# Expert outputs weighted by slot and summed by accumulating stores, in a one-layer mixture-of-experts backbone kernel

## What is computed

```python
g_prob = softmax(t @ wg + bg)                 # 4 groups, the best one is taken
e_prob = softmax(e_logits of that group)      # 4 experts in it, the best two are taken
w = g_p * e_p / sum(e_p)                      # gate of each choice
hid = t @ w_exp_in[e]; a, up = split(hid)     # (1024 x 512) for each of 16 experts
y = (silu(a) * up * gate) @ w_exp_out[e]      # (256 x 1024)
x = layer_norm(ALPHA * x + gf * sum_of_two_y, ln2_g, ln2_b)
```

## Time and profile before

| | |
|---|---|
| runs | 552.16 us median of 3 (551.97 to 552.78) |
| profiled execution, first to last instruction | 550.5 us |
| what lies around the span, median minus span | 1.7 us |
| PE / DVE / ACT / POOL busy | 509.6 / 437.4 / 273.5 / 98.9 us |
| expert turns | about 356 to 509 us, some 9.35 us each |
| last normalisation | about 507 to 550 us |

### The profile page before, as it was taken

The page is one execution under the profiler, slowest core; times in us unless marked ns, Lnnn a source line. Parts: engine busy times, 40 slices in busy tenths (PEclk is TensorE's granted clock), DMA queues, the critical chain, the costliest instruction groups (busy, mean ns, idle before and its releaser), DMA issues.

```text
span 550.5 us, 8091 instructions
## 1 busy us (share of the span) xinstructions
PE 509.6 (93%) x3137; PEld 421.5 (77%) x3138; DVE 437.4 (79%) x703; ACT 273.5 (50%) x378; POOL 98.9 (18%) x114
## 2 busy tenths in 40 slices
PE   4999999999999997999999999999999999998670
PEld 1579999997799995777787788877888888886220
DVE  3217899989798803998559879989999999996984
ACT  2336412002031313997712224767888888884373
POOL 0005800003000001232000000212624242312201
PEclk9999999999999999999999999999999999999786
DMA  8997995729876551228188209989999999998667
GB/s 298 387 386 242 232 349 184 240 79 279 320 245 233 173 134 41 59 60 230 41 298 340 89 39 338 422 321 397 387 391 388 375 384 370 375 310 311 252 190 157
DMA packets 56831, 142.36 MB, mean 259 GB/s; under 512 B 8375, under 2 KB 17138, under 8 KB 50904
## 3 DMA queue, kind: packets, MB, share of 16 engines
q1 hardware_dynamic: 44792, 119.06, 60.3%
q0 software_dynamic: 9120, 20.80, 12.9%
q10 hardware_dynamic: 2880, 1.98, 1.2%
HBM read 129.71 MB, written 20.20 MB: 272 GB/s over the span
## 4 chain that ended last, share of the span: by engine, by line
PE 64%; DVE 18%; issue 7%; DMA 5%; ACT 3%; SPq 1%; DVEq 0%; POOL 0%; ACTq 0%; POOLq 0%
PE PS L1861 9%; PE PS L1863 9%; PE PS L1862 9%; PE PS L1959 8%; PE PS L1960 8%; PE PS L1964 8%; DVE PS L1391 2%; DMA uni<-in_w_ada 2%; PE PS L2266 2%; DMA g<-x_rows 2%; DVE w_lo L1525 2%; PE PS L2380 2%; DVE uni L1407 2%; ACT uni L948 1%; PE PS L2194 1%
## 5 line engine op out<-in xcount | busy, mean ns | idle before, releaser
L1861 PE MATMUL PS<-w_hi,act_hi 128*128 128x512 f32 x244 | 98.7, 405 | 0.9 <-DVE act_lo L1619 0.9
L1959 PE MATMUL PS<-act_hi,w_hi 128*128 128x320 f32 x320 | 97.6, 313 | 0.2 <-issue 0.2
L1960 PE MATMUL PS<-act_lo,w_hi 128*128 128x320 f32 x320 | 96.3, 309 | 0.0
L1863 PE MATMUL PS<-w_hi,act_lo 128*128 128x512 f32 x244 | 95.4, 391 | 0.0
L1862 PE MATMUL PS<-w_lo,act_hi 128*128 128x512 f32 x244 | 95.2, 390 | 0.0
L1281 DVE SCALAR_TENSOR_TENSOR uni<-raw,uni 128x512 f32<-128x512 f32 x112 | 75.1, 743 | 0.0
L1964 PE MATMUL PS<-act_hi,w_lo 128*128 128x320 f32 x320 | 72.9, 309 | 0.0
L1959 PEld LDWEIGHTS PS<-act_hi,w_hi 128*128 128x128 f32 x320 | 60.1, 188 | 4.2 <-issue 3.2
L1960 PEld LDWEIGHTS PS<-act_lo,w_hi 128*128 128x128 f32 x320 | 60.1, 188 | 0.0
L803 ACT ACTIVATE w_hi<-raw 128x2048 fp32r<-128x2048 f32 x14 | 26.4, 1915 | 58.5 <-PE PS L1964 48.3
L1861 PEld LDWEIGHTS PS<-w_hi,act_hi 128*128 128x128 f32 x244 | 45.9, 188 | 11.8 <-issue 1.9
(11 more groups left out here) (285 smaller groups left out, 934.2 us busy)
## 6 DMA issues: line engine op xcount, KB each, us to landing
raw<-in_w_ada SPq DMA_DIRECT2D x20, 1024.0 KB, 7.6
raw<-in_w_expert_in SPq DMA_DIRECT2D x16, 1024.0 KB, 11.8
uni<-in_w_expert_out SPq DMA_DIRECT2D x15, 1024.0 KB, 11.1
raw<-in_w_in SPq DMA_DIRECT2D x12, 1024.0 KB, 8.3
g<-in_w_expert_in SPq DMA_DIRECT2D x8, 1024.0 KB, 12.0
uni<-expert_rows SPq DMA_DIRECT2D x10, 512.0 KB, 7.2
uni<-in_w_ada SPq DMA_DIRECT2D x4, 1024.0 KB, 14.5
raw<-in_w_out SPq DMA_DIRECT2D x4, 1024.0 KB, 6.2
```

Of the source, the lines that this page charges most:

```text
L1861: T.matmul(out, lh, rh, start=first, stop=False)
L1863: return T.matmul(out, ll, rh, start=False, stop=last)
L1959: T.matmul(out, a, h_hi[:, k, sl], start=f, stop=False)
L1960: T.matmul(out, a, h_lo[:, k, sl], start=False, stop=False)
```

## The change

- The router's gates are computed earlier (`token_gates` in turn 0) and stored to a small DRAM array (`gate_dram`); for each expert POOL gathers the gates of its list entries into a column of `slot_gate` (`gather_gates`), and ACT's copy out of PSUM scales each row by it.
- `y_dram` becomes one array of 640 rows. SP zeroes it before attention. The expert stores add to it by token number.
- The expert in turn p is number (p % 4) * 4 + p // 4, so that the experts of a group are four turns apart, and the router's expert columns are permuted to match (also the bias, by one copy).
- Tokens are numbered with stride: token p of tile n is row 5p + n of `h2_dram` and `y_dram`.
- The end loads one row for each token (five loads), `weight_rows` and `add_rows` are gone, and the centring of a tile comes two tiles after its gating.

```diff
-    PAGE = 1024
+    PAGE = TOK
+        gate_dram = dram("choice_gates", (2 * PAGE, 1))
-        y_dram = dram("expert_rows", (2 * PAGE, D))
+        y_dram = dram("expert_rows", (TOK, D))
+        EXPERT = [(p % NG) * EG + p // NG for p in range(NE)]
+            sp.wait_ge(s_nb, 1)
+            for n in range(NT):
+                sp.dma_start(dap(y_dram, n * D, [[NT * D, P], [PAST, D // PAST], [1, PAST]]),
+                             no_bias.unsqueeze(1).to_broadcast([P, D // PAST, PAST])).then_inc(s_yz, 16)
             x1_away(1)
             expert_out(1)
+            sp.wait_ge(s_gt, 1)
+            sp.dma_start(dap(gate_dram, 0, [[NT, P], [PAGE, 2], [1, NT]]), gates[:, :, :]).then_inc(s_gd, 16)
             expert_in(5, 0)
-                for c in range(2):
-                    r0 = c * PAGE + t * P
-                    sp.dma_start(fin_y[:, n, c, :], y_dram[r0:r0 + P, :]).then_inc((s_fy, s_fy2)[c][n], 16)
+                sp.dma_start(fin_y[:, n, 0, :], dap(y_dram, n * D, [[NT * D, P], [1, D]])).then_inc(s_fy[n], 16)
+            def gather_gates(c):
+                if c == 0:
+                    pool.wait_ge(s_lc, 2)
+                    pool.wait_ge(s_gd, 16)
+                pool.indirect_dma_start(slot_gate[:, c:c + 1], None, gate_dram,
+                                        bass.IndirectOffsetOnAxis(ap=list_d[:, c:c + 1], axis=0),
+                                        bounds_check=2 * PAGE - 1, oob_is_err=False).then_inc(s_sg[c % 2], 16)
             def store_rows(c):
                 if c == 0:
-                    pool.wait_ge(s_lc, 2)
+                    pool.wait_ge(s_yz, 16 * NT)
                 pool.wait_ge(s_ya, c + 1)
-                pool.indirect_dma_start(y_dram, bass.IndirectOffsetOnAxis(ap=list_d[:, c:c + 1], axis=0), y_sb[:, c % 2, :], None,
-                                        bounds_check=2 * PAGE - 1, oob_is_err=False).then_inc(s_yst[c % 2], 16)
+                pool.indirect_dma_start(y_dram, bass.IndirectOffsetOnAxis(ap=list_s[:, c:c + 1], axis=0), y_sb[:, c % 2, :], None,
+                                        bounds_check=TOK - 1, oob_is_err=False, compute_op=ALU.add).then_inc(s_yst[c % 2], 16)
                 if 4 <= c < NE + 3:
                     store_rows(c - 4)
+                if 2 <= c < NE + 2:
+                    gather_gates(c - 2)
-                nc.scalar.activation(y_sb[:, b, :], PS[:, 6:8, :].rearrange("p a n -> p (a n)"), ACT.Copy).then_inc(s_ya, 1)
+                act.wait_ge(s_sg[b], 16 * (c // 2 + 1))
+                nc.scalar.activation(y_sb[:, b, :], PS[:, 6:8, :].rearrange("p a n -> p (a n)"), ACT.Copy,
+                                     scale=slot_gate[:, c:c + 1]).then_inc(s_ya, 1)
             expert_ohi(0)
             nc.scalar.activation(small[:, 100:101], eps, ACT.Tanh)
+            act.wait_ge(s_d12, 1)
+            nc.scalar.activation(uni[:, 9340:9340 + NG * NT], uni[:, 9340:9340 + NG * NT], ACT.Exp)
+            nc.scalar.activation(uni[:, 9360:9360 + NT], uni[:, 9360:9360 + NT], ACT.Exp).then_inc(s_d12, 1)
             half_tanh(0, 0)
             gathered_hi(1, 1)
             expert_whi(2, 0)
             act_hi_copy(0, 0)
-            act.wait_ge(s_d12, 1)
-            nc.scalar.activation(uni[:, 9340:9340 + NG * NT], uni[:, 9340:9340 + NG * NT], ACT.Exp)
-            nc.scalar.activation(uni[:, 9360:9360 + NT], uni[:, 9360:9360 + NT], ACT.Exp).then_inc(s_d12, 1)
...
-            act.wait_ge(s_slot, 1)
-            for n in range(3):
-                weight_rows(n)
             for n in range(NT):
-                if n == NT - 1:
-                    scaled_rows(n - 1)
                 squares(n)
                 deviation(n)
-                if n + 3 < NT:
-                    weight_rows(n + 3)
-                if 1 <= n < NT - 1:
-                    scaled_rows(n - 1)
+                if n >= 2:
+                    scaled_rows(n - 2)
+            scaled_rows(NT - 2)
...
+            V.memset(small[:, 8:25], 0.0)
             link(V.memset(uni[:, 5120:5200], 0.0))
+            dve.wait_ge(s_wrl, 64)
+            link(V.tensor_copy(rb[:, E_AT:NR].rearrange("p (j g) -> p g j", g=NG),
+                               logits[:, 0, 0:NE].rearrange("p (g j) -> p g j", g=NG)))
...
             silu_times_up(0, 0)
+            token_gates()
             gathered_lo(1, 1)
...
-            add_rows(0)
-            for n in range(NT + 1):
-                if n < NT:
-                    gate_rows(n)
-                    mean(n)
-                if n + 1 < NT:
-                    add_rows(n + 1)
-                if 1 <= n < NT:
-                    inverse(NT + n - 1)
-                    centred(n - 1)
+            for n in range(NT):
+                gate_rows(n)
+                mean(n)
+                if 2 <= n < NT - 1:
+                    final_inverse(n - 2)
+                    centred(n - 2)
+            last_residual()
+            for n in (NT - 3, NT - 2):
+                final_inverse(n)
+                centred(n)
             last_tile()
```

More of the change, by code:

```diff
@@ L1168, in _ @@
                     act.wait_ge(s_y, i + (NE + 1))
-                    nc.scalar.activation(y_sb[:, 1, :], PS[:, 6:8, :].rearrange("p a n -> p (a n)"), ACT.Copy).then_inc(s_ya, 1)
-            def weight_rows(n):
-                act.wait_ge(s_fy[n], 16)
-                y1 = fin_y[:, n, 0, :]
-                nc.scalar.activation(y1, y1, ACT.Copy, scale=gates[:, 0, n:n + 1]).then_inc(s_fg, 1)
+                    nc.scalar.activation(y_sb[:, 1, :], PS[:, 6:8, :].rearrange("p a n -> p (a n)"), ACT.Copy,
+                                         scale=over_gate).then_inc(s_ya, 1)
             def scaled_rows(n):
@@ L1656, in _, with token_gates @@
             for h in range(2):
-                V.tensor_scalar(list_last[:, h:h + 1], PS[:, 7, NE - 1:NE], 2.0, 2.0 * AWAY + h, ALU.mult, ALU.add)
+                link(V.tensor_scalar(list_t[:, NE + h:NE + h + 1], second[:, NE - 1:NE], 2.0, 2.0 * AWAY + h, ALU.mult, ALU.add))
+                V.scalar_tensor_tensor(out=list_last[:, h:h + 1], in0=PS[:, 7, NE - 1:NE], scalar=2.0,
+                                       in1=list_t[:, NE + h:NE + h + 1], op0=ALU.mult, op1=ALU.add)
             V.tensor_scalar(list_d[:, 0:NE], PS[:, 7, 0:NE], AWAY, None, ALU.add).then_inc(s_lc, 1)
+            def token_gates():
+                dve.wait_ge(s_d12, 2)
+                gw = rs[:, 170:170 + 3 * NT].rearrange("p (a t) -> p a t", a=3)
+                link(V.tensor_reduce(gw[:, 0, :], gexp, AX.X, ALU.add))
+                link(V.scalar_tensor_tensor(out=gw[:, 1, :], in0=d12, scalar=1.0, in1=gw[:, 0, :], op0=ALU.add, op1=ALU.mult))
+                link(V.reciprocal(gates[:, 0, :], gw[:, 1, :]))
+                V.tensor_tensor(gates[:, 1, :], gates[:, 0, :], d12, ALU.mult).then_inc(s_gt, 1)
             silu_times_up(0, 0)
+            token_gates()
             gathered_lo(1, 1)
@@ L1743, in overflow_table @@
                 link_over(V.tensor_scalar(over_f, over_f, float(NE - 1), None, ALU.min))
-                V.tensor_copy(over_i[:, 1:1 + MORE], over_f).then_inc(s_hot, 1)
-            LATER = {3: chunk_count, 4: token_slots, 5: token_gates}
+                number, less = rs[:, 140:140 + MORE], rs[:, 150:150 + MORE]
+                link_over(V.tensor_scalar(number, over_f, float(EG), None, ALU.mult))
+                for first in range(NG, NE, NG):
+                    link_over(V.tensor_scalar(less, over_f, float(first), 1.0 - NE, ALU.is_ge, ALU.mult))
+                    link_over(V.tensor_tensor(number, number, less, ALU.add))
+                V.tensor_copy(over_i[:, 1:1 + MORE], number).then_inc(s_hot, 1)
+            LATER = {3: chunk_count, 4: token_slots}
             for c in range(NE):
@@ L1785, in _ @@
                     act_lo_sub(i + NE, 1)
-            def add_rows(n):
-                dve.wait_ge(s_fg, n + 1)
-                dve.wait_ge(s_fy2[n], 16)
-                y1, y2 = fin_y[:, n, 0, :], fin_y[:, n, 1, :]
-                V.scalar_tensor_tensor(out=y1, in0=y2, scalar=gates[:, 1, n:n + 1], in1=y1,
-                                       op0=ALU.mult, op1=ALU.add).then_inc(s_fs, 1)
             def gate_rows(n):
-                dve.wait_ge(s_fs, n + 1)
+                dve.wait_ge(s_fy[n], 16)
                 y1 = fin_y[:, n, 0, :]
@@ L2410, in constants @@
     row = np.concatenate([
-        np.arange(NE) // 4, np.arange(NE), NE * CAP - CAP - np.arange(NE) * CAP]).astype(np.float32)
-    tiles = np.repeat(np.array([NT - 1] + list(range(NT - 1))) * P, 2) + np.tile([0, 1024], NT)
-    tok = tiles[None, :] + np.arange(P)[:, None] - 8192
+        np.arange(NE) % 4, np.arange(NE), NE * CAP - CAP - np.arange(NE) * CAP]).astype(np.float32)
+    tiles = np.repeat(np.arange(NT), 2) + np.tile([0, NT * P], NT)
+    tok = tiles[None, :] + np.arange(P)[:, None] * NT - 8192
+    fold = np.eye(P, dtype=np.float32).reshape(P, 4, 32)[:, :, 0:24].sum(1)
```

(1 more changed line is left out.)

77 lines of the change are left out of this document (43 added, 34 removed).

## The result

The changed kernel takes 571.67 us (median of 4 runs, 570.7 to 572.7), the kernel before 552.08 us beside it. The ratio is 1.0353 with an interval of 1.0329 to 1.0378: 19.6 us slower. The prediction was 563.2 with 553 to 569: right in its direction and in what it said bounds the kernel, too low by 8.5 us and outside its range. The profiled execution has a span of 570.3 us, 19.8 more than before.

What follows compares the result with a forecast made beforehand. PE and DMA both bound the expert turns, PE by rate, DMA by a backlog without slack at its end. Turns 12.0 us later less 1.0 gained at the end, +11.0 on 552.2, gave 563.2 us, range 553 to 569.

Steps and rivals of the forecast that it cites:

- A backlog in the weight queue without slack at its end: Expert turns: weight loads land ever later after issue, 6.6 us then 17.7, and only 2.8 us of 112 was idle.
- adding stores at twice the price: Expert stores: an added byte costs over twice a plain one, 5.50 against 2.57 us per MB of DMA time.
- ACT's waits for output weights: Sign in the late expert turns: ACT idles for DMA before reading output weights, turns over 9.35 us.
- the whole engine time of q0: Extra DMA work of 14 stores before the last x1 rows, 1.14 us a turn with gates: 16.0 us.
- the gates' own packets: Expert turns: 80 small gate packets a turn cost 0.18 us of all DMA engines.
- 14 x 1.14 = 16.0 us of work go into a queue that had about 4 us of idle: Expert turns: the added DMA work fills the idle time first, so x1 rows and DVE's last stage come 12.0 us later.
- the start's stall: Before turn 3's rows: POOL waits for the gate store, PE stands 3.8 us, swallowed by the later DMA delay.
- The check from the other side: Output weights of turn 13: 11.5 stores before them, 13.1 us less 2.8 idle, delay PE by 10.3 us.
- only the stall: Rival, chance 0.17: weight queue uses engines during adding stores' waits, leaving stall 3.8 less end 1.0: +2.8, 555.0 us.
- The end: After the last x1 rows: DVE's last multiply comes 3.6 us earlier, but adding output stores leave 1.0 us gained.
- faster: Rival, chance 0.12: adding stores cost nothing beside loads and the end keeps its full 3.6 us: 548.6 us.
- the result buffers: Rival, chance 0.11: y_copy waits for stores landing after 20 us, binding from 16.8: +17.6, 569.8 us.

Runs made afterwards that it cites:

- Experiments 1: Changed kernel with its expert stores plain instead of adding, each overwriting its row: 555.44 us, ratio 1.0067.
- experiment 2: Kernel before with adding expert stores and its two result pages zeroed first, nothing else of the change: 568.06 us, ratio 1.0297.
- experiment 7: Changed kernel, two edits: output weights of turns 3 to 14 on ScalarE's queue, 572.84 us; input weights of turns 10 to 12 ahead of output weights, 572.66 us.
- (6): Changed kernel with only some expert stores adding: even turns and last halves 564.86 us, turns 0 to 6 562.71 us, turns 7 to 14 564.55 us.
- experiment 3: Changed kernel without the gate store and gate gathers, every slot scaled by 0.5: 568.01 us, ratio 1.0289.
- experiment 4: Changed kernel with the gate gathers of turns 0 and 1 issued behind the row gather of turn 3: 570.38 us, ratio 1.0358.
- experiment 8: The four output stores plain instead of adding, shift missing: in the changed kernel 566.29 us, in the kernel before 549.20 us.

## Why the prediction was right in kind and 8.5 us short

**Right: what bounds, and what the change loads onto it.** A backlog in the weight queue without slack at its end, adding stores at twice the price, and ACT's waits for output weights as the sign of it: all are there. The price per store (0.96 said, 1.05 measured) and the whole engine time of q0 (16.0 said, 15.7 measured) came out, the whole in part by luck: the stores were priced 1.3 us too low over 14 turns and the gates' own packets some 1.4 too high. Experiments 1 and 2 show it from both sides, 16.2 us taken away and 16.7 us put in.

**The step that failed: "14 x 1.14 = 16.0 us of work go into a queue that had about 4 us of idle", hence +12.0.** The idle time was counted as room that the new work would fill. It was not filled, it grew by 3.9 us: a swing of 7.9 us (6 by the second execution in the ledger). With the 1.3 us by which the weight packets became dearer, and 0.3 less for q0, this is the whole way from 12.0 to 20.9. In such a loop the idle time need not be room: a load is issued only when the compute engines have read its slot, and when these wait for a late load the next issues come late as well, as at 432 to 436. That is what the trace shows at that place; that all of the idle time comes from it was not shown, and its cause stays open. The two other orders of loads that were tried do not give it back (experiment 7), and the late adding stores have it without the early ones (6). By the ledger 1.9 us of the growth come with the gates already when the stores are plain, and 2.0 to 4.1 with the adding stores, where two executions can differ by 1.8. Whether uneven shares of the 16 engines are part of it was not tried.

**Too small: the gates.** 0.18 us a turn was worked out from their own packets. Without the gates the kernel takes 3.7 us less, 0.26 a turn. Of q0's time they take 1.1 us, 0.08 a turn; the rest is q1's time or the start's stall (experiment 3).

**Unseen: the restart at the lower clock.** After two of the five waits, at 436 and at 480, PE's granted clock is 0.57 over 4 us, and after the start's stall 0.52 to 0.62. The prediction priced a stall by its length alone. Since the engine time sets the end, it isn't shown that this costs anything by itself.

**The check from the other side looked at one place.** It took the output weights of turn 13 as the point where lead runs out, and they were only the last. All later ones of turn 5 on have some 14 us between issue and use in one queue with loads that have 20 to 27; the first delay shows there.

**Not shown: that the start's stall is swallowed.** The prediction took its 3.8 us as hidden by the later lag. The ledger of experiment 3 fits this, and experiment 4, meant to test it, has a stall of its own. With plain stores the time is 555.44 us, and the rival "only the stall" gave 555.0. That is luck: its sum was a stall of 3.8 us, and the trace has one of 3.0 us on PE and 4.6 us of waits for output weights besides. The stall's path had a part that the prediction left out: ACT's first copy waits 4.5 us for its gates.

**The end: the number by luck.** 1.0 us of gain was predicted and 1.1 measured. But the sum was 3.6 us won and 2.6 lost to the adding output stores, and the runs have 5.4 won and 4.3 lost, of which 3.1 are lost with plain outputs too (experiment 8). Nor do SP's halves stand until the adding stores are through, as the prediction read in 540 to 546: in the changed kernel both queues move from 564 to 566 (0.26 MB of q0 beside 0.24 of q1), while 0.05 MB of q1 moved in the 2 us before.

**The rivals.** "Only the stall" falls by q0's price, "faster" falls with it, and "the result buffers" by landings of at most 14.3 us, under their 16.8.

## What to carry to other kernels

Where DMA engines are busy to 97%, price a new transfer by what its kind costs the engines (here an adding store costs twice a plain one), and charge it in full: here the few per cent that were idle took up none of the new work, they grew. Before such a change, do its dearest part alone in the old kernel; experiment 2 would have told most of the result for one edit. Moving the late load to another queue only chose who waits. And after an edit that is to take a stall away, look in its trace whether the stall is gone.

## What the runs showed of the hardware

An indirect store that adds, 80 rows of 4 KB, costs 1.05 us more of all 16 engines than the plain one, at the same packets and bytes (within 1%), and lands only 1.9 us later (median 11.5 against 9.6 us).

A gather of 4 bytes for each of 80 slots holds POOL for 1.0 to 3.1 us and lands after 9.3 us (median). That is about as long as a plain store of 0.33 MB takes (9.6).

Whether GpSimd's add of two SBUF operands holds up a DVE instruction goes by DVE's operands. A multiply with both inputs in SBUF takes 2.78 instead of 1.22 us beside it, and an operation of one column 2.18 instead of 0.16. The centring, which reads one input from PSUM, keeps its 1.28 us (at 541.12, beside an add that starts at 541.26). The Trainium skill (SBUF — State Buffer, "Who interferes with whom") says that a VectorE instruction with two SBUF inputs contends with a GpSimd instruction that reads SBUF, and one with a single SBUF input doesn't. The trace agrees in both.
